# Expert outputs scattered in one group of eight over six PSUM banks, modulation blocks moved to where fillers stood, and the final transposes made before the final scale is known

## The reference

```python
# every layer, for context (own modulation) and latent tokens
mods = (silu(cvec) @ w_mod + b_mod)            # 6 vectors of 1024: sh1, sc1, g1, sh2, sc2, g2
h = rmsnorm(x, ln1_g) * (1 + sc1) + sh1
z = h @ w_in                                   # conv | attention q,k,v | mLSTM q,k,v,o | 16 gates
conv_o = cb * short_conv(cc * ch, conv_w)
na_o   = attention(...)                        # 4 heads of 64; neighbourhood window + context keys
ml_o   = mlstm_readout(mlstm_bidir(...), mo, ml_norm_g)   # 4 heads of 128, two directions
x = x + g1 * (concat(conv_o, na_o, ml_o) @ w_out)
h2 = rmsnorm(x, ln2_g) * (1 + sc2) + sh2
x = x + g2 * hier_moe(h2, ...)                 # 16 experts of 512, top group, top 2 in it
# at the end
y = rmsnorm(x, final_g)
# further outputs: new keys and values, new mLSTM states of the context tokens
```

## Time and profile before

| | |
|---|---|
| median of 3 runs | 1279.57 us (1273.12 to 1284.75) |
| the profiled execution | 1278.14 us, span from first to last instruction 1276.3 us |
| mean granted TensorE clock | 0.975 of full speed |
| busy | PE 92%, VectorE 33%, ScalarE 20%, Pool 3% |
| DMA | 315.16 MB, mean 247 GB/s |
| chain that ended last | PE 76%, VectorE 10%, DMA 9% |

### The profile page before, as it was taken

One profiled execution on the slowest core, in us unless ns is written; L12 is line 12 of the kernel. 1 busy time (PEld: TensorE's weight loads), 2 busy tenths in 40 slices (PEclk: granted clock), 3 DMA queues, 4 the chain that ended last, 5 costly groups with the idle time before them and its releaser, 6 DMA issues.

```text
span 1276.3 us, 15287 instructions
## 1 busy us (share of the span) xinstructions
PE 1177.5 (92%) x6238; PEld 615.8 (48%) x6238; DVE 426.9 (33%) x1169; ACT 249.1 (20%) x511; POOL 44.3 (3%) x70
## 2 busy tenths in 40 slices
PE   3999999899989999999989998999998999999994
PEld 3545555585444534443334564557544443443332
DVE  4411041454441333222261203136444142322226
ACT  2210121242221111110041012116222111111012
POOL 1500000000030000000000000000000000000000
PEclk8999999999999899999999999999998989999996
DMA  9965333495239899999771554125521979999961
GB/s 318 323 229 202 140 132 132 147 349 157 91 101 414 342 358 411 388 371 409 303 263 66 176 210 151 56 104 205 155 93 69 413 310 382 414 384 371 414 274 50
DMA packets 95513, 315.16 MB, mean 247 GB/s; under 512 B 5980, under 2 KB 6352, under 8 KB 86608
## 3 DMA queue, kind: packets, MB, share of 16 engines
q1 hardware_dynamic: 91856, 306.43, 63.1%
q0 software_dynamic: 3584, 7.71, 2.3%
HBM read 310.92 MB, written 4.99 MB: 248 GB/s over the span
## 4 chain that ended last, share of the span: by engine, by line
PE 76%; DVE 10%; DMA 9%; ACT 2%; issue 2%; SPq 0%; DVEq 0%; ACTq 0%
PE ps L897 15%; PE ps L1294 14%; PE ps L907 8%; DMA ring<-in_w_up 7%; PE ps L1344 7%; PE ps L1065 5%; PE ps L1132 5%; PE ps L856 3%; PE ps L1160 3%; DMA ring<-in_w_mod 1%; PE ps L846 1%; PE ps L1161 1%; PE ps L1184 1%; PE ps L1221 1%; PE ps L1096 1%
## 5 line engine op out<-in xcount | busy, mean ns | idle before, releaser
L1294 PE MATMUL ps<-ring,arena 128*64 128x512 f32 x816 | 241.0, 601 | 7.5 <-DMA ring<-in_w_up 7.5
L1941 DVE SCALAR_TENSOR_TENSOR xT<-ps,modT,xT 128x128 f32<-128x128 f32 x320 | 116.7, 412 | 242.4 <-PE ps L1161 150.4
L897 PE MATMUL ps<-ring,hT 128*128 128x512 f32 (+1 forms) x480 | 194.9, 565 | 0.0
L897 PEld LDWEIGHTS ps<-ring,hT 128*128 128x128 f32 x480 | 90.7, 190 | 97.9 <-issue 94.6
L1344 PE MATMUL ps<-ring,arena 128*64 128x512 f32 x384 | 118.2, 609 | 8.1 <-ACT arena L1609 8.1
L1294 PEld LDWEIGHTS ps<-ring,arena 128*64 128x64 f32 x816 | 65.2, 136 | 106.8 <-issue 106.8
L907 PE MATMUL ps<-hT,ring 128*128 128x384 f32 x320 | 106.2, 490 | 0.0
L1294 PE MATMUL ps<-slot,arena 128*64 128x512 f32 x208 | 101.4, 601 | 2.4 <-DMA slot<-in_w_up 2.4
L1065 PE MATMUL ps<-mixT,ring 128*128 128x384 f32 x256 | 83.4, 487 | 1.5 <-ACT mixT L1537 1.5
L2159 DVE SCALAR_TENSOR_TENSOR y_low<-ps,route,y_high 128x512 fp32r<-128x512 f32 x32 | 24.0, 751 | 167.5 <-ACT y_high L1615 166.7
L907 PEld LDWEIGHTS ps<-hT,ring 128*128 128x128 f32 x320 | 59.9, 190 | 40.6 <-issue 0.8
(11 more groups left out here) (314 smaller groups left out, 1273.1 us busy)
## 6 DMA issues: line engine op xcount, KB each, us to landing
ring<-in_w_up SPq DMA_DIRECT2D x56, 1024.0 KB, 9.6
ring<-in_w_gate SPq DMA_DIRECT2D x54, 1024.0 KB, 12.9
ring<-in_w_down SPq DMA_DIRECT2D x52, 1024.0 KB, 9.6
ring<-in_w_mod SPq DMA_DIRECT2D x24, 2048.0 KB, 12.6
ring<-in_w_in SPq DMA_DIRECT2D x14, 2048.0 KB, 9.1
slot<-in_w_down SPq DMA_DIRECT2D x16, 1024.0 KB, 9.8
slot<-in_w_gate SPq DMA_DIRECT2D x14, 1024.0 KB, 13.1
slot<-in_w_up SPq DMA_DIRECT2D x12, 1024.0 KB, 7.3
```

Source lines behind the costliest of these rows:

```text
L897: mm = pe.matmul(p[:, 0:n], hT[:, k, t * P:(t + 1) * P], w[:, k, c0:c0 + n], start=(k == 0), stop=(k == KT - 1))
L1294: mm = pe.matmul(out[which][64 * s:64 * s + 64, :], xg[:, k, cols[s]], w[i][:, k % 4, :], start=(k == 0), stop=(k == KT - 1))
L1941: ins = dve.scalar_tensor_tensor(xT[:, m, cols], p[:, cols], modT[:, L, gate0 + m, j:j + 1], xT[:, m, cols], ALU.mult, ALU.add)
```

## The change

Scatters: all eight of a pair come after k = 4 (`BACK_GROUPS`), over six banks in the order 6, 7, 4, 5, 0, 1 (`BACK_BANKS`); so do the job's. The scatters after the last pair of a layer keep banks 6 and 7. TensorE waits for all eight drained tiles before the job's `lselT` (bank 0) and for the last job tile before `selT` of pair 2. VectorE makes all eight additions before the product of gate and up, where it made two after it.

Mixing: the fifth block goes ahead of `context_turn`, two go behind values 2 and 5, the eighth ahead of `turn_probs(7)` (before: behind values 1, 3, 5, 7), and in the first layer one block each before reads 1, 3, 5, 7 (before: 0, 1, 2, 3). The fillers of `context_turn` and `turn_probs(7)` go from 3 products to 1.

Norms: VectorE adds only squares 0 to 6; the last goes into PSUM by a second product. At the start of the second layer, and at the end, Pool adds them in VectorE's place.

End: each tile of the last scatter is scaled with `final_g` as soon as its residual is done (even tiles on ScalarE, odd ones on VectorE) and transposed behind scatters 4 to 7 and after; the sum of squares is made for tokens in rows (three columns), root and reciprocal work on 128 x 3, and the copies out of PSUM apply the scale.

```diff
 # mixing_steps
-              ("turn", 5), ("turn", 6), ("turn", 7), ("scores", 1), ("context_turn",)]
-    del mods[:4]
+              ("turn", 5), ("turn", 6), ("turn", 7), ("scores", 1)] + mods[4:5] + [("context_turn",)]
+    del mods[:5]
     for n in range(8):
+        if n == 7:
+            steps += mods[:1]
+            del mods[:1]
...
-        steps += [("values", n)] + (mods[:1] if n % 2 else [])
-        if n % 2:
+        steps += [("values", n)] + (mods[:1] if n in (2, 5) else [])
+        if n in (2, 5):
...
-        steps += ([("decay", dh + 1)] if dh < 7 else []) + mods[:1] + [("read", dh)]
+        steps += mods[:1] if dh % 2 else []
+        steps += [("read", dh)]
...
-                bk.place(("back", j - 1, m), 6 + m % 2)
+                bk.place(("back", j - 1, m), BACK_BANKS[m % len(BACK_BANKS)])
+BACK_BANKS = (6, 7, 4, 5, 0, 1)
+BACK_GROUPS = {4: range(0, 8)}
...
 # Pool
+                if not ly.first:
+                    for k in range(1, KT - 1):
+                        pool.wait_ge(ly.squares_ready, k + 1)
+                        if k > 1:
+                            pool.wait_ge(ly.summed_ready, k - 1)
+                        pool.tensor_tensor(squares[0][:, 0, :], squares[0][:, 0, :], squares[0][:, k, :], ALU.add
+                                           ).then_inc(ly.summed_ready, 1)
...
 # TensorE
-                    pe.wait_ge(ly.summed_ready, (n + 1) * (KT - 1))
-                    done(pe.matmul(p[:, 0:NT], mean, squares[n][:, 0, :], start=True, stop=True), ("ss", n))
+                    pe.wait_ge(ly.summed_ready, (n + 1) * (KT - 2))
+                    pe.matmul(p[:, 0:NT], mean, squares[n][:, 0, :], start=True, stop=False)
+                    pe.wait_ge(ly.squares_ready, (n + 1) * KT)
+                    done(pe.matmul(p[:, 0:NT], mean, squares[n][:, KT - 1, :], start=False, stop=True), ("ss", n))
...
-                    keep_busy(p, 3)
+                    keep_busy(p, 1)
...
-                        keep_busy(p, 1 if n == 0 else 3)
+                        keep_busy(p, 1)
...
 # TensorE, pair j (job_products alike)
+                        for m in BACK_GROUPS.get(k, ()) if j > 0 else ():
+                            if j == JOB_AFTER + 1:
+                                job_scatter(m)
+                            else:
+                                scatter(j - 1, m)
                     if j == JOB_AFTER + 1:
-                        job_scatter(6)
-                        job_scatter(7)
-                    elif j > 0:
-                        scatter(j - 1, 6)
-                        scatter(j - 1, 7)
+                        ly.wait_loop_dve(pe, ("lback", BACK_ORDER[-1]), 0)
...
 # TensorE, the end
+                    for t in range(TILES):
+                        mm = pe.transpose(ps[2 * t + k // 4][:, (k % 4) * P:(k % 4 + 1) * P],
+                                          fin_scaled_rows[:, k, t * P:(t + 1) * P], ident)
...
                 for m in range(KT):
                     scatter(PAIRS - 1, m)
+                    if m >= 4 and ly.number == DEPTH - 1:
+                        turn_out(m - 4)
...
+                pe.matmul(ps[6][:, t:t + 1], mixT[:, 0, t * P:(t + 1) * P], mean[:, 0:1], start=(t == 0), stop=False,
...
 # ScalarE, the end
+                if k % 2 == 0:
+                    act.activation(fin_scaled_rows[:, k, :], xT[:, k, :], ACT.Copy,
...
-            act.activation(std[:], ps[0][:, 0:NT], ACT.Sqrt, bias=eps).then_inc(fin_root, 1)
+            act.activation(small[:, 40:43], ps[6][:, 0:3], ACT.Sqrt, bias=eps).then_inc(fin_root, 1)
+            act.wait_ge(fin_root, 2)
+            act.wait_ge(fin_turned, KT)
...
+                act.activation(fin_rows[:, t, 512:1024], ps[2 * t + 1][:, :], ACT.Copy, scale=small[:, 40 + t:41 + t]
...
 # VectorE
-                for k in range(KT):
+                for k in range(KT if ly.first else 0):
                     sum_square(0, k)
...
-                    for m in range(6 if j > 0 else 0):
+                    for m in range(KT if j > 0 else 0):
                         add_back(last, m)
+                        if j == PAIRS and ly.number == DEPTH - 1 and m in (2, 4, 6):
+                            scale_out(m - 1)
...
-            dve.reciprocal(std[:], std[:]).then_inc(fin_root, 1)
+            dve.reciprocal(small[:, 40:43], small[:, 40:43]).then_inc(fin_root, 1)
...
+                dve.tensor_scalar(fin_rows[:, t, 0:512], ps[2 * t][:, :], small[:, 40 + t:41 + t], None, ALU.mult
```

More of the change, by code:

```diff
@@ L109, in mixing_steps @@
     for dh in range(8):
-        steps += ([("decay", dh + 1)] if dh < 7 else []) + mods[:1] + [("read", dh)]
-        del mods[:1]
+        steps += [("decay", dh + 1)] if dh < 7 else []
+        steps += mods[:1] if dh % 2 else []
+        steps += [("read", dh)]
+        if dh % 2:
+            del mods[:1]
     assert not mods
@@ L285 @@
 JOB_BANK = {"lxg": 3, "lgu": 2, "lselT": 0, "laT": 1, "ly": 5,
-            **{("lback", m): 6 + n % 2 for n, m in enumerate(BACK_ORDER)}}
+            **{("lback", m): BACK_BANKS[n % len(BACK_BANKS)] for n, m in enumerate(BACK_ORDER)}}
 def slot_of(n):
@@ L822, in _ @@
                     pool.dma_start(relb[:], bias_windows[d + 1]).then_inc(layers[d + 1].relb_loaded, 16)
+            for k in range(1, KT - 1):
+                pool.wait_ge(fin_sq, k + 1)
+                if k > 1:
+                    pool.wait_ge(fin_summed, k - 1)
+                pool.tensor_tensor(mixT[:, 0, :], mixT[:, 0, :], mixT[:, k, :], ALU.add).then_inc(fin_summed, 1)
         @block.tensor
@@ L1187, in job_products @@
                             mm.then_inc(ly.loop_full, 1)
-                        if 1 <= k <= 6:
-                            scatter(JOB_AFTER, k - 1)
-                    scatter(JOB_AFTER, 6)
+                        for m in BACK_GROUPS.get(k, ()):
+                            scatter(JOB_AFTER, m)
+                    for m in range(8):
+                        bk.wait_drained(pe, ("back", JOB_AFTER, m))
                     p = ps[JOB_BANK["lselT"]]
@@ L1194, in job_products @@
                     mm.then_inc(ly.loop_full, 1)
-                    scatter(JOB_AFTER, 7)
                     ly.wait_loop_dve(pe, "lgu", 0)
@@ L1215, in job_scatter @@
                         ly.wait_loop_act(pe, "ly", 0)
-                    if n < 2:
-                        bk.wait_drained(pe, ("back", JOB_AFTER, 6 + n))
+                    depth = len(BACK_BANKS)
+                    if n < depth:
+                        bk.wait_drained(pe, ("back", JOB_AFTER, KT - 1))
                     else:
-                        ly.wait_loop_dve(pe, ("lback", BACK_ORDER[n - 2]), 0)
+                        ly.wait_loop_dve(pe, ("lback", BACK_ORDER[n - depth]), 0)
                     rows_of = slice(64 * (m // 4), 64 * (m // 4) + 64)
@@ L1351, in _, with turn_out @@
                         job_products()
+                def turn_out(k):
+                    if k % 2:
+                        pe.wait_ge(fin_scaled, k // 2 + 1)
+                    else:
+                        pe.wait_ge(fin_scaled_act, k // 2 + 1)
+                    for t in range(TILES):
+                        mm = pe.transpose(ps[2 * t + k // 4][:, (k % 4) * P:(k % 4 + 1) * P],
+                                          fin_scaled_rows[:, k, t * P:(t + 1) * P], ident)
+                    mm.then_inc(fin_turned, 1)
                 for m in range(KT):
                     scatter(PAIRS - 1, m)
-            pe.wait_ge(fin_summed, KT - 1)
-            pe.matmul(ps[0][:, 0:NT], mean, mixT[:, 0, :], start=True, stop=True).then_inc(fin_sum, 1)
-            for i in range(6):
-                pe.wait_ge(fin_scaled, 4 * (i % 2) + 4)
-                for n in range(4):
-                    mm = pe.transpose(ps[1 + i][:, n * P:(n + 1) * P],
-                                      hT[:, (i % 2) * 4 + n, (i // 2) * P:(i // 2 + 1) * P], ident)
-                mm.then_inc(fin_turned, 1)
+                    if m >= 4 and ly.number == DEPTH - 1:
+                        turn_out(m - 4)
+            for k in range(4, KT - 1):
+                turn_out(k)
+            layers[-1].bk.wait_drained(pe, ("back", PAIRS - 1, 6))
+            pe.wait_ge(fin_summed, KT - 2)
+            for t in range(TILES):
+                pe.matmul(ps[6][:, t:t + 1], mixT[:, 0, t * P:(t + 1) * P], mean[:, 0:1], start=(t == 0), stop=False,
+                          skip_group_check=True)
+            pe.wait_ge(fin_sq, KT)
+            for t in range(TILES):
+                mm = pe.matmul(ps[6][:, t:t + 1], mixT[:, KT - 1, t * P:(t + 1) * P], mean[:, 0:1], start=False, stop=True,
+                               skip_group_check=True)
+            mm.then_inc(fin_sum, 1)
+            turn_out(KT - 1)
         @block.scalar
@@ L2117, in add_back, with scale_out @@
                         residual(("back", after, m), 40, m, full_of(("back", after, m)))
+                def scale_out(k):
```

(9 more changed lines are left out.)

33 lines of the change are left out of this document (10 added, 23 removed).

## The result

The changed kernel takes 1264.28 us (median of 9 runs, 1262.4 to 1268.85), the kernel before 1283.55 in the runs beside it (1273.12 to 1287.99). The ratio is 0.987, 95% interval 0.9847 to 0.9894: 1.3% faster, 16.7 us by the ratio, where 2.2% was forecast. 1264 lies in the range given, by 0.7 us, but over a third of the forecast gain is missing. The profiled run took 1262.4 us, its span is 1260.3 (1276.3 before).

A forecast was written before the change was run, and what follows sets the result against it. TensorE, busy 92%, was taken as the bound, with DMA a close second limit in the expert stage. Grouping -11, blocks and fillers -3.3, norms -1.9 and end -11.5 sum to -27.7 us: 1251 us, range 1237 to 1265.

The forecast's parts named there:

- How much of the 13.5 stays?: Expert stage: of 13.5 us a layer saved on TensorE by grouped scatters, 5.5 stays after w_up waits, 11 in all.
- rival 5: Decay stage: TensorE idles around the last probabilities, the clock stays at 1.2 GHz, up to 28 us a layer, 1306; chance 0.04.
- What bounds the kernel: Expert stage: TensorE and DMA limits a few per cent apart; DMA's unused share, about 14 us, caps any TensorE saving.
- Six banks, additions: Scatter group: six banks let eight scatters run at 0.35 us each; VectorE's additions, some 6.5 us, cost nothing.
- rival 4: Scatter group: VectorE comes late, scatters go at 0.8 us instead of 0.35, +16 instead of -11, 1278; chance 0.04.
- Blocks and fillers: Attention and decay stages: moved modulation blocks and cut fillers give -3.3 us, bounds -5 and +2.
- the context's gain: Before the context transposes: a block replaces filler work and covers a bank wait, 1.9 + 0.5 us second layer, 1.9 first.
- Norms: Start of the second layer: Pool adds six squares, TensorE starts at filler's end, -1.9 us; middle norms 0 within 0.4.
- The end: After the last scatters: scaling and turning run under the last scatter, end at 1264.8, -11.5 us, bounds -9 and -13.5.
- the same 3.05: Kernel's tail: from the last copy to the end of the span still takes 3.05 us, as before.
- rival 3: End and norm: Pool and VectorE block each other a whole addition, 3 us more at the end, 1257; chance 0.08.
- Rival 1: Expert stage: DMA takes back all of the grouping, every pair becomes a waiting one, -16.7 us, 1262; chance 0.14.

## Why the prediction was right and wrong, point by point

Of the 10.5 us between the forecast and the means, 6.0 lie in the expert stages, 2.0 in the attention stages, 1.3 at the end, 1.0 between output projection and first pair, 0.2 in the norm.

**The step that failed** is in the scatter group, "How much of the 13.5 stays?", at "I take 5.5 a layer, 11 in all". The two halves that it named were nearly right: TensorE saves 13.5 (some 14.5 by the sums above), and the waits for w_up take back 8.0 of a layer's saving by the forecast (6.8 in the four waiting pairs and 1.2 in the late ones), 7.1 and 8.0 measured. With TensorE kept busy in these waits the stages gave 6.4 each. What the step left out is that a wait of 2.4 or 3.1 us does not only cost itself: the granted clock can fall to 0.50 behind it, as at three of seven waits here, and the next steps run at 1.2 GHz. The forecast had this mechanism as rival 5 and put it at the wrong place, the decay stage, because it looked for idle time where fillers were cut and not where waits grow. With it the grouping shortens the stages by 1.0 and 4.0 in the mean (4.0 and 4.8 in the changed kernel's own profile), so 11 became about 5, and 3.7 (1.5 to 6.0) when the grouping was timed alone.

**What bounds the kernel.** Right: seven places with a load of w_up, the hole behind the job, and a saving that these limit. Not seen was the cheap way out that the same reading offers. The text says that "the whole group now lies behind that wait"; ahead of it the group is free, and that is worth 15 us.

**Six banks, additions.** Right: the scatters of a group run at 0.35 each, so rival 4 (0.8 each) doesn't occur.

**Blocks and fillers,** -3.3 forecast, -1.3 by the means (-0.3 and -1.0), and 2.5 in timing, within its uncertainty. Right: the context's gain, where the clock stays up, and the read-out's wait of 2 us. Wrong: "In the decay stage blocks only change places among busy TensorE work". At read-out 7 the turned block needs VectorE's copy while VectorE is still in the read-outs' chain, and the work that hid it before is spent. Of the 3.4 us that the kernel with the blocks put back gains in this stretch, 1.8 is the first read-out's wait, which was forecast; the rest goes with the turned block, whose wait falls from 2.65 to 0.90, and with the clock behind it. In layer 2 the clock can fall ahead of the context transposes: the block took 3.63 us there, and 1.96 in the kernel with the old norms, which has the same code in this place. The first layer's stretch from output projection to first pair is 0.8 longer in the mean of the kernels with the new blocks (79.5 with the old norms, 78.6 with the old blocks, but 78.7 with the old end); its cause was not tried.

**Norms,** -1.9 forecast, -1.3 in the pair of profiles, -1.7 by the means. Pool is the limit, not the filler: the sum waits 0.40 for Pool's sixth addition. The page of the profile gives 1.00 us for an addition, near the upper bound of 1.03 where I took 0.9, and 0.14 us pass between two additions, which I had not counted. By the Trainium skill (GPSIMD Engine Reference, Performance versus the Vector engine) it was an estimated 0.85 to 0.9; the measurement decides. The middle norm's zero held: 0.5 us more at its sum, 0.4 less just ahead of it.

**The end,** -11.5 forecast, -10.6 in the profile, -10.2 by the means, 9 timed. The order of work was right. The term off is "the same 3.05" from the last copy to the end of the span: the copies end at 1255.99 and the span 4.3 later. The three rows' stores are now issued 0.66 us apart, where it was 1.7, and from issue to landing they take 2.7, 3.3 and 3.9 us, where each took 2.6. VectorE against Pool was there, and small: the scaling at 1244.36, issued 0.12 us behind the start of a Pool addition, took 1.10 us, the other three 0.41 or 0.42. In the seven profiles with this end one or two of the four scalings took 0.8 to 1.1 us, and up to three of Pool's six additions took 1.1 to 1.2 in place of 1.00. So the rule of the Trainium skill (SBUF — State Buffer, Who interferes with whom) agrees with the trace in kind, but rival 3, by which each scaling pays a whole addition, does not hold.

**Rivals and chances.** Rival 1 gave 1262, close to the 1264 measured, but by another way: pairs 2, 4 and 5 don't wait, and it has no clock in it. That it is faster by over 1% was right. The range held by 0.7 us, which is luck: the forecast's own range (1244 to 1258) did not, and of the bounds in it none stood for the clock in the expert stage.

## What to carry to other kernels

When saved work ends ahead of a wait for a load, ask what stands on each side of that wait: independent work is free ahead of it and costs its full length behind it, and here one k step's difference in its place was worth 15 us, nearly as much as the whole change (16.7). Price a wait that grows with the clock that may fall behind it, not with its own length alone; work of no use in the wait can then pay for itself. And where the clock is a toss, compare a stage over several profiles before a microsecond in it is explained.

## What was not expected of the hardware

- The clock falls or stays in the same code from one profile to the next, in kernels that differ elsewhere: a block of 64 short products took 1.96 or 3.41 us, and the first layer's expert stage 267.7 to 273.2 us with 13.7 to 27.3 us at the lower level.
- Fillers in waits of 2.4 to 3.1 us, on an engine that has nothing to do there, made the kernel some 6.5 us faster.
- Six dependent additions on Pool took 6.72 us, 1.15 from one start to the next, for 1.00 of work each.
